# PEER activations of the last 32 tokens by gathered expert rows, their coefficients carried by the gate batches

## The reference, cut to what matters

```python
def peer(h, w_query, sub_keys, expert_u, expert_v):      # 8 heads, top 16, 128 keys
        q = (xb @ w_query).reshape(t, PEER_HEADS, 2, PEER_HALF).astype(jnp.float32)
        scores = jnp.einsum('thpd,hpnd->thpn', q, sk)
        s_val, s_idx = lax.top_k(scores, PEER_TOPK)
        cand = s_val[:, :, 0, :, None] + s_val[:, :, 1, None, :]
        c_val, c_idx = lax.top_k(cand.reshape(t, PEER_HEADS, PEER_TOPK * PEER_TOPK), PEER_TOPK)
        ...
        expert = i1 * N_KEYS + i2
        gate = jax.nn.softmax(c_val, axis=-1)
        act = jax.nn.gelu(jnp.einsum('thkd,td->thk', expert_u[expert], xb).astype(jnp.float32))
        coef = (gate * act).astype(xb.dtype)
        return jnp.einsum('thk,thkd->td', coef, expert_v[expert])
```

## Time and profile before

| | us |
|---|---|
| median of 3 runs | 2859.18 |
| the profiled execution's own time | 2859.4 |
| its span, first to last instruction | 2857.6 |
| PE busy | 2832.9 (99%) |
| DVE busy | 2279.5 (80%) |
| ACT busy | 1016.2 (36%) |
| POOL busy | 741.1 (26%) |

### The profile page before, as it was taken

The page is one execution under the profiler, slowest core; times in us unless marked ns, Lnnn a source line. Parts: engine busy times, 40 slices in busy tenths (PEclk is TensorE's granted clock), DMA queues, the critical chain, the costliest instruction groups (busy, mean ns, idle before and its releaser), DMA issues.

```text
span 2857.6 us, 39744 instructions
## 1 busy us (share of the span) xinstructions
PE 2832.9 (99%) x14646; PEld 1531.0 (54%) x14742; DVE 2279.5 (80%) x4300; ACT 1016.2 (36%) x1347; POOL 741.1 (26%) x518
## 2 busy tenths in 40 slices
PE   9999999999999999999999999999999999999998
PEld 5456555556666444444544455555566664444443
DVE  6955899997888899999501248999978888999996
ACT  2253232335555333333321232223345553333332
POOL 0000233331112454544000002323211115445450
PEclk9999999999999999999999999999999999999999
DMA  4213687867997999999321236787679979999993
GB/s 157 88 47 142 241 294 264 306 243 270 321 309 296 396 391 395 398 396 401 109 88 59 76 142 232 273 295 279 240 284 311 310 288 399 395 391 398 398 399 140
DMA packets 214691, 775.99 MB, mean 272 GB/s; under 512 B 15492, under 2 KB 101896, under 8 KB 194600
## 3 DMA queue, kind: packets, MB, share of 16 engines
q1 hardware_dynamic: 49952, 416.87, 38.3%
q0 software_dynamic: 73728, 268.47, 25.5%
q10 hardware_dynamic: 90888, 89.14, 9.1%
HBM read 681.88 MB, written 92.54 MB: 271 GB/s over the span
## 4 chain that ended last, share of the span: by engine, by line
PE 86%; issue 5%; PEld 4%; DMA 2%; DVE 1%; ACT 1%; DVEq 0%; PEldq 0%; POOL 0%; SPq 0%; ACTq 0%
PE ps L1772 23%; PE ps L1703 11%; PE ps L1702 11%; PE ps L1701 11%; PE ps L1675 8%; PE ps L1371 5%; PEld ps L1772 4%; PE ps L1362 4%; PE ps L1392 4%; PE ps L1754 2%; PE ps L1753 2%; DMA arena<-in_ur,arena 1%; PE ps L1711 1%; PE ps L1486 1%; PE ps L1425 0%
## 5 line engine op out<-in xcount | busy, mean ns | idle before, releaser
L1772 PE MATMUL ps<-arena 128*128 128x512 bf16 x4512 | 990.7, 379 | 7.9 <-DVE arena L1246 1.8
L492 POOL DMA_INDIRECT arena<-in_ur,arena x256 | 346.6, 1354 | 1592.2 <-DVE arena L1084 935.5
L1772 PEld LDWEIGHTS ps<-arena 128*128 128x128 bf16 x4608 | 450.4, 98 | 547.1 <-ACT arena L710 2.7
L1057 DVE TENSOR_TENSOR arena<-arena 128x1024 bf16<-128x1024 f32 x512 | 611.7, 1220 | 118.5 <-ACT arena L710 96.3
L1703 PE MATMUL ps<-xnh,arena 128*128 128x384 bf16 x2048 | 667.6, 326 | 0.0
L1702 PE MATMUL ps<-xnl,arena 128*128 128x384 bf16 x2048 | 667.5, 326 | 0.0
L1701 PE MATMUL ps<-xnh,arena 128*128 128x384 bf16 x2048 | 667.4, 326 | 0.0
L710 ACT ACTIVATE arena<-arena 128x1024 bf16<-128x1024 f32 x512 | 524.3, 1048 | 117.8 <-PE ps L1772 96.8
L492 POOL DMA_INDIRECT arena<-in_v,arena x256 | 393.7, 1538 | 406.0 <-DVE x_res L1093 345.4
L1093 DVE SCALAR_TENSOR_TENSOR x_res<-arena,x_res 128x1024 f32<-128x1024 f32 x256 | 328.5, 1283 | 20.8 <-issue 0.5
L736 ACT ACTIVATE arena<-ps 128x384 f32<-128x384 f32 x256 | 125.8, 491 | 565.3 <-PE ps L1703 565.2
(11 more groups left out here) (206 smaller groups left out, 2286.4 us busy)
## 6 DMA issues: line engine op xcount, KB each, us to landing
arena<-in_v SPq DMA_DIRECT2D x64, 2048.0 KB, 10.2
arena<-in_u SPq DMA_DIRECT2D x62, 2048.0 KB, 10.3
h_scratch<-arena ACTq DMA_DIRECT2D x60, 768.0 KB
arena<-h_scratch SPq DMA_DIRECT2D x60, 768.0 KB, 8.6
arena<-gate_scratch SPq DMA_DIRECT2D x64, 640.0 KB, 6.8
arena<-in_wmix SPq DMA_DIRECT2D x14, 2048.0 KB, 7.9
gate_scratch<-xnT ACTq DMA_DIRECT2D x10, 2048.0 KB
gate_scratch<-arena ACTq DMA_DIRECT2D x10, 2048.0 KB
```

The lines of the kernel that those rows point to most:

```text
L492: pool.indirect_dma_start(ring[n % NBUF], None, ur_d[L] if g < P else vr_d[L], at).then_inc(gat_in[n % NBUF], 16)
L1057: dve.tensor_tensor(lo[:, s], raw[s // TPG][:, s % TPG], hi[:, s], ALU.subtract).then_inc(lo_ready, 1)
L1772: last = pe.matmul(ps[:, 2 + 2 * tt + dh], c, v[:, TPG * s + q, dh * 512:(dh + 1) * 512], start=start and c is ch and v is hi, stop=stop a ...
```

## The change

For the last 32 tokens (partitions 96 to 127 of tile 3) `h` is no longer formed on PE: the matmuls of `tile` run over `TU` = 352 columns and not 384. Their activations come from gathered rows of `expert_u` as tile 0's do: four picks (`EXJ`) of 32 tokens (`EX`) fill the 128 partitions, so 32 more gathers and dots per layer. The expert numbers have to be moved to the other partitions for this: DVE writes them in two small instructions per head, POOL moves them with three small DMAs (`shift`), and four DMAs copy the 32 tokens' rows to the four quarters. The gathers of both kinds stand in one list, `U_JOBS`. Gelu of the 32 columns is ACT's, four DMAs bring them back to partitions 96 to 127, DVE multiplies them into the gates (`extra_gates`), PE turns these and DVE puts them where the last four gate batches read (`extra_turned`). In the `h` of these 32 tokens stand ones (`memset` of `hst`), so that gate times `h` is the coefficient. The places of `dots` and `sums` change with it, and `HG_GROUP` becomes 7. SP waits for the last extra dot before it loads the first gates, since the 32 tokens' rows lie in that buffer.

```diff
-HG_GROUP = 4
+HG_GROUP = 7
+EX = 32
+TU = TD - EX
+EXJ = P // EX
+EXK = TOPK // EXJ
+E_LO = P - EX
+U_JOBS = []
+for _h in range(4):
+    U_JOBS += [("main", _h * TOPK + _k) for _k in range(TOPK)] + [("extra", _h * EXK + _k) for _k in range(EXK)]
+U_JOBS += [("extra", 4 * EXK + _k) for _k in range((PH - 4) * EXK)]
+U_JOBS += [("main", 4 * TOPK + _k) for _k in range((PH - 4) * TOPK)]
+NU = len(U_JOBS)
+JOBS = NU + P
...
+                sp.wait_ge(hg_ex_ready, L + 1)
                 gates_load(NG - 2, 0)
...
+            def shift(L, h):
+                pool.wait_ge(e_ready_ex, 2 * (PH * L + h + 1))
+                at = slice(h * EXK, (h + 1) * EXK)
+                for j in range(EXJ - 1):
+                    pool.dma_start(eidx_ex[j * EX:(j + 1) * EX, at], e_move[E_LO:P, j, at]).then_inc(shift_in[h % 2], 16)
+            def rows_for_extras(L):
+                pool.wait_ge(xs_ready, TT * (2 * L + 2))
+                for j in range(EXJ):
+                    pool.dma_start(xg_ex[j * EX:(j + 1) * EX], xs[E_LO:P, TT - 1]).then_inc(xg_ex_in, 16)
+            def gathers(L):
+                rows_for_extras(L)
+                shifts = {U_JOBS.index(("main", h * TOPK)): h for h in range(4)}
+                shifts.update({U_JOBS.index(("extra", (h - 1) * EXK)): h for h in range(4, PH)})
+                for i in range(JOBS):
+                    if i in shifts:
+                        shift(L, shifts[i])
+                    gather(L, i)
...
+                    if n == B0 + 16:
+                        act.wait_ge(hg_ex_ready, L + 1)
+                        act.activation(hg_ex, hg_ex, ACT.Gelu_apprx_tanh).then_inc(hg_ex_act, 1)
+                    if n == B0 + 17:
+                        act.wait_ge(hg_ex_act, L + 1)
+                        for j in range(EXJ):
+                            act.dma_start(act_ex[E_LO:P, j], hg_ex[j * EX:(j + 1) * EX]).then_inc(act_ex_in, 16)
...
+                dve.tensor_tensor(xg_ex, xg_ex, gbc, ALU.mult)
+                for q in range(2):
+                    dve.memset(hst[q][:, :, TU:TD], 1.0).then_inc(h_ones, 1)
...
-                    dots(3 if h else 0)
+                    dots(4 if late else 3 if h else 0)
...
-                    dots(2 if late else 0)
+                    dots(2 if late else 1 if h else 0)
...
-                    dots(1 if late else 0)
+                    dots(1 if h else 0)
... (three places)
+                    dve.scalar_tensor_tensor(e_move[E_LO:P, :, near], moved[0], float(NK), moved[1],
+                                             ALU.mult, ALU.add).then_inc(e_ready_ex, 1)
+                    dve.scalar_tensor_tensor(eidx_ex[E_LO:P, near], mine[0][:, (EXJ - 1) * EXK:], float(NK), mine[1][:, (EXJ - 1) * EXK:],
+                                             ALU.mult, ALU.add).then_inc(e_ready_ex, 1)
...
                 for n in range(11, 13):
                     ahead(NK // 2 + n)
+                    dots(3)
...
                     elif B0 <= n < NK - 2:
                         dots(2)
+                    elif n < B0:
+                        dots(1)
...
-                        sums(4)
+                        sums(5 if k % 2 else 4)
...
-                        pe.matmul(ps[:, j % 2, 0:TD], uh, xnh[:, kd], start=kd == 0, stop=False)
+                        pe.matmul(ps[:, j % 2, 0:TU], uh, xnh[:, kd, 0:TU], start=kd == 0, stop=False)
... (all three matmuls)
+                pe.wait_ge(coef_ex, L + 1)
+                pe.transpose(ps[:, 6, 0:EX], gt[E_LO:P, TT - 1], ident[E_LO:P, E_LO:P]).then_inc(coef_ex_tr, 1)
```

106 lines of the change are left out of this document (78 added, 28 removed).

## The result

The kernel after takes 2978.04 us (median of 4 runs, 2975.88 to 2982.26), the kernel before 2858.89 us beside it (4 runs, 2857.48 to 2861.03). The ratio is 1.0418, with a 95% interval of 1.0400 to 1.0436. Forecast were 2920 us, +61; measured are +119, above the range's upper end of 2944. The direction was right, the size was not.

What follows compares the result with a forecast made beforehand. PE was taken as the bound, with DVE within 2 to 3% in the heads and `expert_v` groups. Per layer -2.5 + 32.8 = +30.3 us; two layers, +60.6 on 2859.4, gave 2920 us, 8-in-10 range 2844 to 2944.

Steps and rivals of the forecast that it cites:

- Stretch 4: Groups of `expert_v`: rows of five sums and a 2.05 us wait of the single sum behind add 32.8 us per layer.
- Stretch 3: Tiles 77 to 127, the gate batches: PE stays the bound and 51 narrower tiles save 16.3 us per layer.
- Stretch 1: Heads 1 to 6: head 1 starts 1.7 us earlier, DVE is the bound, head 7 starts 3.7 us later.
- Stretch 2: Head 7 to the first gate batch: more dots and 8 us of gather waits bring PE's first batch at +13.8 us.
- 5 us for this and 3 us for the ring of five: Behind head 7: 5 us for gathers queued behind small DMAs, 3 us for five buffers feeding eleven dots.
- The small DMAs: On POOL before head 7's gathers: three, between 0 and 2 us each, taken as 1.2 us.
- Room enough: Rival: DVE's 13.1 us idle before the batches takes the dots without waits; faster, 2834 to 2851 us; chance 0.17.
- PE throughout: Rival: PE stays the bound everywhere, 82 us saved over both layers, 2777 us; chance 0.04.
- Worse than the sum: Rival: waits feed on each other, gathers take 10 us and more; +45 us per layer, 2950 us; chance 0.11.
- The forecast's own range: Total time of 2892 to 2942 us, with the `expert_v` groups costing +20 to +40 us per layer.

Runs made afterwards that it cites:

- run 2: Kernel before with 352 columns instead of 384 in the dense matmuls and the gelu, the last 32 tokens' activations left out: 2806.07 us, ratio 0.9814.
- Run 11: Kernel before with the head dots of the kernel after (13 for 12, 8 for 4 in head 7), no extra rows: 2883.79 us, ratio 1.0074.
- run 12: Kernel after, but in every fourth tile ACT takes the gelu ahead of the split that may wait for a load: 3011.71 us, ratio 1.0551.
- run 8: Kernel after with dots up to the first batch as before, one dot per batch tile, four sums per group, HG_GROUP 6: 2861.54 us, ratio 1.0007.
- run 7: Kernel after without the 11 dots between heads and first batch, a dot in every batch tile instead of every second: 2985.87 us, ratio 1.0445.

## Why the forecast was right in direction and wrong in size

**Stretch 4, the groups of `expert_v`: right.** Forecast +32.8 us, measured +34.6 in layer 0 and +35.2 in layer 1. The wait taken at 2.05 us was 2.2 to 3.0 in layer 0. The split into periods of 16.7 and 17.4 was wrong, 19.1 and 15.2 came, because the single sum falls into the same span from `low` to `low` as the five sums ahead of it; the pair, 34.25, is near the 31.08 + 2.9 = 33.98 forecast. Of the two prices weighed there, 8.0 us and more by the trace and 3.2 us by the Trainium skill ("DMA: Bandwidth & Descriptors", anatomy of one DMA), the rows of after say 6.2 to 10.4: the skill's figure would have put this stretch at +8.2.

**Stretch 3, the batches: nearly right.** Forecast -16.3, measured -11.5. Half of the missing 4.8 us is 2.41 us of PE before the first product. Another 1.55 us stand right behind PE's wait of 9.65 us, where the first batch and its tile take 6.05 us and the following ones 4.50. PE's timeline there:

```profile
708.23 0.50 PE L1802 MATMUL ps<-xnh,arena 128*128 128x352 bf16 x1
708.52 0.50 PE L1803 MATMUL ps<-xnl,arena 128*128 128x352 bf16 x1
...
712.30 0.31 PE L1803 MATMUL ps<-xnl,arena 128*128 128x352 bf16 x1
712.45 0.31 PE L1804 MATMUL ps<-xnh,arena 128*128 128x352 bf16 x1
```

The step from one matmul to the next is 0.29 us and then 0.15: PE ran at the lower level of its clock at first. The rest, 0.8 us, I can't place.

**Stretch 1, heads 1 to 6: the step that failed first.** It said "2 us of waits for gathers" and a head 1 that starts 1.7 us earlier. Head 1 started 1.6 us later, because head 0 itself started 4.1 us late (278.6 for 274.5), behind a wait of 4.08 us for ACT. From head 0 to head 1 it is 43.7 us, 2.5 less than before, as in run 2, which has no extra rows at all. DVE did wait 6.1 us for the layer's first gathers there (before 4.2), but ACT's copy of the scores, without which head 1 can't start, ended just then. Its row in ACT's timeline, and DVE's split behind it:

```profile
320.06 1.02 ACT L807 ACTIVATE arena<-ps 128x1024 f32<-128x1024 f32 x1 [0.19 <-PE ps L1812]
321.11 1.23 DVE L1121 TENSOR_TENSOR arena<-arena 128x1024 bf16<-128x1024 f32 x1
```

In the profiled executions of runs with the same instructions up to head 0, it starts at 276.1 to 281.3 us, so a part of the 4.1 is chance; why all of them are later than the 274.5 of before stays open. The prediction had put the new product and the two memsets at nothing; they stand ahead of head 0. The waits for gathers within the six heads were 7.5 us. The rest of the stretch was right: from head 1's start to head 7's it grew by 11.0 us, which is 6 x (1.14 + 0.27 - 0.85) = 3.4 plus 7.5. So 3.3 + 5.5 = 8.8 us are the error, and it is a size.

**Stretch 2, head 7 to the first batch: the step that failed most.** It said "5 us for this and 3 us for the ring of five"; measured are 18.1 us of waits for gathers, 10 more. The work was right: head 7 grew by 4.9 (forecast 4.9), and 12.6 us of dots stood against 13.1 us of waits. The lateness of +32.9 is the forecast +13.8, plus 3.3, 5.5 and 10.1, up to 0.2 us. One kind of term, the wait for gathers ahead of the batches, was put at 10 us and is 25.6. With head 1's 3.3 us it is these 19 us, and stretch 3's 4.8 and stretch 4's 1.8, that layer 0 lacked: 56.0 measured for 30.3. In layer 1 the same points lack 33 us (first batch +38 for +13.8), together the 58 us between 2920 and 2978.

Why was it so small? I took the landing time of a stage without bursts, 8.6 to 10.4 us, and counted one queueing per place. The gathers ahead of the batches share the DMA with 2 MB loads of `u`, and come in bursts after POOL has waited at head 7's small DMAs: there they took up to 13.2 us, and 13.0 the second one behind the small DMAs. Run 11 shows that it takes no extra rows for waits in the heads, only dots closer together. What makes one gather land in 5 us and the next in 13 is not shown; the loads of `u` and the gathers' own number are both there. Each late dot also puts DVE's splits back, which frees the buffers of `u` later; whether this chain by itself adds time no run shows, since run 12 changed more than that.

**The small DMAs: dearer on paper than on the chip.** The prediction gave 1.2 us to each of three ahead of head 7's gathers. Three of them took POOL 1.58 us together (the row at 648.60). The price is not their time but what they wait for, head 7's picks, with other gathers behind them. No run without that wait was made, so its share of the 18.1 us stays open.

**The rivals.** "Room enough" failed where it said it would: `expert_v` costs more than the dense stage gives, and the dense stage gives nothing. "PE throughout" is priced by run 2: even without any work on DVE it would be 2806 and not 2777. "Worse than the sum" names what happened (waits that feed on each other, gathers of 10 us and more), with +45 us per layer; measured are +59.6. I gave it 0.11, and the range's end of 2944 lay below its 2950. That choice of the range is the other error: a rival whose mechanism I could not price should have been inside it. The forecast's own range has a slip too: -2.5 with +20 to +40 per layer is 2894 to 2934 us, and not 2892 to 2942.

## What to carry to other kernels

Before adding work to an engine that feeds on a ring of prefetched buffers, count how many buffers it empties between two places where the ring can fill, and price each turn by the slowest landing in that stage, not the median (even the slowest of before, 10.4 us, was too little here, where 13.2 came); behind a row of five uses in this ring of five, the next use had only the time of that row to hide a whole transfer. Where two engines are within 3% of each other, moving work from one to the other pays no more than the slack of the second, stage by stage: here 28.2 us of 41 per layer were to be had, and 36.5 were spent. The same change, PE's saving included, cost 119 us in one placement and nothing in another (run 8, ratio 0.9995 to 1.0019), so look at the placement before judging the idea.

## What the runs showed of the hardware

The granted clock fell where PE stood still. Windows of PE in after, three stretches of 50 us around the first batch (busy us, instructions, clock, DMA share, GB/s); in the kernel before all three are busy 50.00 at 1.00.

```profile
600.00:650.00 50.00, 39.87 (x245) 0.90 0.60 219
650.00:700.00 50.00, 35.79 (x206) 0.86 0.81 287
700.00:750.00 50.00, 43.46 (x380) 0.90 0.91 313
```

With levels of 2.4 and 1.2 GHz, 0.86 is 28% of the stretch at the lower one. A batch matmul of 128 columns is 0.29 us there at 706.54, against 0.22 before and 0.23 in run 7, where PE had waited only 0.95 us. So a wait of PE can cost a little more than its length, 1.55 us more at the first batch; the prediction counted PE's waits at their length. In the groups of `expert_v` the clock is 0.98 (970 to 1330 us), but there DVE sets the pace, and no cost of it is seen. A small DMA within SBUF on POOL's queue holds POOL about 0.5 us (1.58 for three, at 648.60 in after), a gather of 512 KB 0.93 to 1.99 us (the 25 from 600 to 700 us).
